# Two halves of a standing operand stored in turn, value by value, in a two-network transformer kernel

## The reference: what is computed

```python
def swiglu(h, w_gu, w_down):              # w_gu 1024 x 5632, w_down 2816 x 1024
    gate, up = jnp.split(h @ w_gu, 2, axis=-1)
    return (jax.nn.silu(gate) * up) @ w_down

def squared_relu_mlp(h, w_up, w_down):    # w_up 1024 x 4096, w_down 4096 x 1024
    return jnp.square(jax.nn.relu(h @ w_up)) @ w_down
```

## Time and profile before

| | |
|---|---|
| median of three executions | 1662.71 us (1662.34 to 1662.93) |
| profiled execution | 1661.7 us |
| its span, first to last instruction | 1660.0 us |
| mean granted TensorE clock | 0.998 |
| PE busy | 1624.5 us (98%) |
| DVE busy | 1030.6 us (62%) |
| ACT busy | 810.1 us (49%) |
| mean HBM rate | 170 GB/s |

### The profile page before, as it was taken

One profiled execution on the slowest core, in us unless ns is written; L12 is line 12 of the kernel. 1 busy time (PEld: TensorE's weight loads), 2 busy tenths in 40 slices (PEclk: granted clock), 3 DMA queues, 4 the chain that ended last, 5 costly groups with the idle time before them and its releaser, 6 DMA issues.

```text
span 1660.0 us, 25696 instructions
## 1 busy us (share of the span) xinstructions
PE 1624.5 (98%) x10390; PEld 1440.9 (87%) x10390; DVE 1030.6 (62%) x1059; ACT 810.1 (49%) x998; POOL 148.9 (9%) x117
## 2 busy tenths in 40 slices
PE   8999999999999999999999999978999999999998
PEld 6888887888889888888888998856999999889997
DVE  6554667754547654568455588766765578666564
ACT  6343567544345533456343556354544466444442
POOL 2000123300002100011000132221000000100000
PEclk9999999999999999999999999999999999999999
DMA  8545452364553554455545444321455545325551
GB/s 304 212 158 202 151 201 77 114 251 174 202 201 129 203 202 177 177 184 215 190 165 202 152 189 153 127 77 54 157 198 196 182 153 203 128 104 201 196 183 52
DMA packets 41212, 282.06 MB, mean 170 GB/s; under 512 B 4592, under 2 KB 4720, under 8 KB 7728
## 3 DMA queue, kind: packets, MB, share of 16 engines
q1 hardware_dynamic: 40752, 279.47, 45.7%
q0 software_dynamic: 384, 1.51, 0.2%
HBM read 279.91 MB, written 1.05 MB: 169 GB/s over the span
## 4 chain that ended last, share of the span: by engine, by line
PE 88%; DVE 5%; ACT 3%; POOL 2%; issue 1%; DMA 0%; SPq 0%; POOLq 0%; DVEq 0%; ACTq 0%
PE ps L393 28%; PE ps L397 27%; PE ps L396 27%; DVE w_lo L1743 1%; PE ps L597 1%; POOL arena L2489 1%; ACT arena L1578 1%; ACT arena L1576 1%; DMA raw<-weights 0%; PE ps L522 0%; PE ps L701 0%; ACT w_hi L1267 0%; ACT arena L1588 0%; DVE stat L2184 0%; PE ps L1054 0%
## 5 line engine op out<-in xcount | busy, mean ns | idle before, releaser
L1743 DVE TENSOR_TENSOR w_lo<-raw,w_hi 128x2048 fp32r<-128x2048 f32 x261 | 594.5, 2298 | 149.9 <-ACT w_hi L1267 149.8
L1267 ACT ACTIVATE w_hi<-raw 128x2048 fp32r<-128x2048 f32 x261 | 491.4, 1908 | 47.5 <-DMA raw<-weights 45.5
L393 PE MATMUL ps<-w_hi,hT 128*128 128x512 f32 (+1 forms) x984 | 384.0, 390 | 9.9 <-DVE hT L1770 7.1
L397 PE MATMUL ps<-w_hi,hT 128*128 128x512 f32 (+1 forms) x984 | 375.0, 381 | 0.0
L396 PE MATMUL ps<-w_lo,hT 128*128 128x512 f32 (+1 forms) x984 | 374.4, 380 | 0.0
L393 PE MATMUL ps<-hT,w_hi 128*128 128x256 f32 x984 | 282.3, 287 | 1.3 <-DVE hT L1770 1.2
L397 PE MATMUL ps<-hT,w_lo 128*128 128x256 f32 x984 | 277.0, 281 | 0.0
L396 PE MATMUL ps<-hT,w_hi 128*128 128x256 f32 x984 | 276.2, 281 | 0.0
L393 PEld LDWEIGHTS ps<-w_hi,hT 128*128 128x128 f32 x984 | 185.9, 189 | 44.4 <-DVE w_lo L1758 7.0
L397 PEld LDWEIGHTS ps<-w_hi,hT 128*128 128x128 f32 x984 | 185.7, 189 | 36.3
L396 PEld LDWEIGHTS ps<-w_lo,hT 128*128 128x128 f32 x984 | 186.2, 189 | 32.0 <-issue 0.7
(11 more groups left out here) (267 smaller groups left out, 1808.8 us busy)
## 6 DMA issues: line engine op xcount, KB each, us to landing
raw<-weights SPq DMA_DIRECT2D x261, 1024.0 KB, 4.8
raw<-weights SPq DMA_DIRECT2D x12, 256.0 KB, 7.1
X<-x SPq DMA_DIRECT2D x4, 256.0 KB, 6.3
out<-X SPq DMA_DIRECT2D x4, 256.0 KB, 2.1
arena<-p POOLq DMA_DIRECT2D x2, 256.0 KB, 5.6
arena<-counts POOLq DMA_DIRECT2D x1, 512.0 KB, 5.0
arena<-nsa_tables POOLq DMA_DIRECT2D x1, 448.0 KB, 6.1
const<-constants SPq DMA_DIRECT2D x1, 300.0 KB, 7.6
```

Source lines behind the costliest of these rows:

```text
L393: mm = nc.tensor.matmul(dst, a_hi, b_hi, start=start, stop=False, skip_group_check=True)
L397: return nc.tensor.matmul(dst, a_lo, b_hi, start=False, stop=stop, skip_group_check=True)
L1267: nc.scalar.activation(unit_cols(w_hi, u, 0, UNIT), raw[:, r * UNIT:(r + 1) * UNIT], ACT.Copy).then_inc(hi_done.sem, 1)
L1743: nc.vector.tensor_tensor(unit_cols(w_lo, u, 0, UNIT), raw[:, r * UNIT:(r + 1) * UNIT], f(unit_cols(w_hi, u, 0, UNIT)), ALU.subtract).then ...
```

## The change

In FFN one and FFN three, `hT` is stored with high and low half in turn: value 0 high, value 0 low, value 1 high, and so on. In the two MLPs `hid` is stored so. `hT_of` and `hid_of` return views with a step of two values (8 bytes) there. The functions `down_tiles`, `down_rows`, `down_rows_last` and the FFN's `up_rows`, as well as the writing of `hid` by ACT and DVE, now take their views from these. FFN two and four, and every other use of `hT` and `hid`, keep the halves apart. Each engine has the same instructions in the same order as before.

Two sizes change besides: `hid` is 24 values longer (and a spacer of 24 values in front of the weights is gone, so that the weights stay where they were, while `const` moves by 96 bytes), and `hT` is 56 values longer, which moves `raw`, `X`, `arena`, `sil` and `spare` by 224 bytes.

```diff
+HID_ROOM, H_ROOM = 40, 72
+H_EVERY_OTHER, HID_EVERY_OTHER = (0, 4), (9, 11)
 MOVE = 16
...
-        hid = sb("hid", 2 * HID + P + MOVE, f32r)
+        hid = sb("hid", 2 * HID + P + HID_ROOM, f32r)
         const = sb("const", NCONST)
-        sb("before_w", 24)
         w_hi, w_lo = sb("w_hi", RING * UNIT, f32r), sb("w_lo", RING * UNIT, f32r)
-        hT = sb("hT", 2 * KC * TOKENS + MOVE, f32r)
+        hT = sb("hT", 2 * KC * TOKENS + H_ROOM, f32r)
...
         def hid_of(s):
 
+            if s in HID_EVERY_OTHER:
+                return hid[:, 0:2 * HID:2], hid[:, 1:2 * HID:2]
...
         def hT_of(s):
 
+            if s in H_EVERY_OTHER:
+                return hT[:, 0:2 * KC * TOKENS:2], hT[:, 1:2 * KC * TOKENS:2]
...
-            def down_tiles(u, h, banks, first=False, last=False):
+            def down_tiles(s, u, h, banks, first=False, last=False):
+                high, rest = hid_of(s)
                 for b in banks:
                     for c in range(HC):
-                        mm = three(out_bank(b), lhs(hid_hi, h + c, b % 2), lhs(hid_lo, h + c, b % 2), unit_cols(w_hi, u, c * DM + b // 2 * 512, 512),
+                        mm = three(out_bank(b), lhs(high, h + c, b % 2), lhs(rest, h + c, b % 2), unit_cols(w_hi, u, c * DM + b // 2 * 512, 512),
...
             def ffn(s, u0):
+
+                h = hT_of(s)
...
-                            mm = three(bank(b0 + tok), lhs(hT_hi, k, tok), lhs(hT_lo, k, tok), unit_cols(w_hi, u, a, 512), unit_cols(w_lo, u, a, 512),
+                            mm = three(bank(b0 + tok), lhs(h[0], k, tok), lhs(h[1], k, tok), unit_cols(w_hi, u, a, 512), unit_cols(w_lo, u, a, 512),
...
-                    nc.scalar.activation(chunk(hid_hi, j % 2 * HC, HC), at(ACT_AT, 512), ACT.Copy).then_inc(hid_hi_done.sem, 1)
+                    nc.scalar.activation(chunk(hid_of(s)[0], j % 2 * HC, HC), at(ACT_AT, 512), ACT.Copy).then_inc(hid_hi_done.sem, 1)
...
-                    nc.vector.tensor_tensor(chunk(hid_lo, h, HC), at(ACT_AT, 512), f(chunk(hid_hi, h, HC)), ALU.subtract).then_inc(hid_split.sem, 1)
+                    nc.vector.tensor_tensor(chunk(hid_of(s)[1], h, HC), at(ACT_AT, 512), f(chunk(hid_of(s)[0], h, HC)), ALU.subtract).then_inc(hid_split.sem, 1)
```

More of the change, by code:

```diff
@@ L550, in down_tiles, with down_rows, down_rows_last @@
                         mm.then_inc(unit_used.sem, 1)
-            def down_rows(u, h, first, t=None):
+            def down_rows(s, u, h, first, t=None):
                 unit_ready(u, t)
                 pe.wait_ge(*hid_split.due(me, turn=t))
-                down_tiles(u, h, range(4), first)
-            def down_rows_last(u, h):
+                down_tiles(s, u, h, range(4), first)
+            def down_rows_last(s, u, h):
                 for i in range(2):
@@ L562, in down_rows_last @@
                     pe.wait_ge(*hid_split.due(me))
-                    down_tiles(u + i, h[i], (0, 2), last=i == 1)
-                down_tiles(u, h[0], (1, 3))
-                down_tiles(u + 1, h[1], (1, 3), last=True)
+                    down_tiles(s, u + i, h[i], (0, 2), last=i == 1)
+                down_tiles(s, u, h[0], (1, 3))
+                down_tiles(s, u + 1, h[1], (1, 3), last=True)
             def ffn(s, u0):
+                h = hT_of(s)
                 def up_rows(us, b0, fresh, t, mid):
@@ L634, in mlp @@
                 up([u0 + 2], 2, 2, None, False, mid={3: lambda: spread(7)}, h=h)
-                down_rows(u0 + 3, 0, True)
+                down_rows(s, u0 + 3, 0, True)
                 u = u0 + 4
@@ L640, in mlp @@
                         up([u + 2 * b], b % 3, 2, None, False, t, h=h)
-                        down_rows(u + 2 * b + 1, (b + 1) % 2 * HC, False, t)
+                        down_rows(s, u + 2 * b + 1, (b + 1) % 2 * HC, False, t)
                 hid_split.due(me, MLP_TURN * (MLP_TURNS - 1))
@@ L644, in mlp @@
                 up([u], 0, 2, None, False, h=h)
-                down_rows(u + 1, HC, False)
-                down_rows_last(u + 2, (0, HC))
+                down_rows(s, u + 1, HC, False)
+                down_rows_last(s, u + 2, (0, HC))
             def columns_t(us, fresh=False, mid={}):
```

## The result

| | before | after |
|---|---|---|
| median of four executions each, us | 1662.53 (1661.15 to 1662.93) | 1671.93 (1670.81 to 1674.12) |
| ratio, 95% interval | | 1.006 (1.0046 to 1.0075) |
| profiled execution, us | 1661.7 | 1670.81 |
| its span, us | 1660.0 | 1669.0 |
| mean granted clock | 0.998 | 0.997 |

The change makes the kernel 9.4 us slower. I had forecast 11.9 us less. The time lies inside my range of 1642 to 1675, but the sign is wrong.

What follows compares the result with a forecast made beforehand. PE, busy for 98% of the span, was taken as the bound. 1776 matmuls at 6.7 ns less gave 1661.7 - 11.9 = 1649.8 us, 1650.8 as a median, other terms 0; range 1642 to 1675 for 8 times in 10.

Steps and rivals of the forecast that it cites:

- My reading: 512-column matmuls: the 13.3 ns excess is the moving stream colliding with the load of the next standing operand; likeliest case 0.60.
- The step that followed from it: FFN one, three and MLPs: a load stepping 8 bytes keeps the stream's pace, collides once, then keeps its distance.
- The term of the sum: 512-column matmuls of FFN one, three and the MLPs: 6.7 ns less each, 1776 times, 11.9 us less.
- at half clock both keep their distance: Matmuls at 1.2 GHz: stream and load run at about the same pace, so the excess is gone there.
- The count: 1776 matmuls affected: FFN one and three 1056, MLPs 768, less the 48 of FFN one's first block.
- More lines, more collisions: Rival, same 1776 matmuls: the strided load touches twice as many places, 13.3 ns more each, 23.7 us, time 1686.4; chance 0.18.
- Nothing changes: Rival, 512-column streams: moving operand and array set the excess, the standing stride doesn't matter; 1662.7 us; chance 0.16.
- The load at half speed: Rival, 50 uncovered places before 512-column groups: a strided load at half speed costs 5.0 us, time 1667.7; chance 0.06.
- my sign of 200: First 256-column matmul before a 512-column group: taking 200 ns or more would show the slow load.
- The 512-column stream covers the load: 512-column matmuls: even a half-speed strided load of 218 ns stays under the 226.7 ns pitch; taken as 0.
- writing with a step is hidden: ACT and DVE writing halves: doubled time uses 1.3 of 4.1 us slack in the MLP; FFNs at most 2.6 us; taken as 0.
- the moved buffers: `const` moved 96 bytes, `arena` and neighbours 224: at most 4.1 us either way over 1366 other matmuls; taken as 0.

Runs made afterwards that it cites:

- stride_at_16: The changed kernel with `hT` and `hid` beginning 16 values further in the four stages, high and low still in turn: 1665.29 us against 1662.05 before, ratio 1.0018.
- ple_at_16: The kernel before with `hT` beginning 16 values further in the two gated projections, where it moves: 1661.03 us against 1662.05, ratio 0.9994 (0.9985 to 1.0003).
- ffn_only: The changed kernel with the stride only in `hT` of FFN one and three, `hid` as before: 1665.95 us against 1662.23 before, ratio 1.0024.
- mlp_only: The changed kernel with the stride only in `hid` of the two MLPs, `hT` as before: 1668.0 us against 1662.23 before, ratio 1.0035.
- aside_8: The changed kernel's sizes, but halves apart and contiguous, beginning 8 values further in the four stages: 1669.75 us against 1662.02 before, ratio 1.0044.
- sizes_only: The changed kernel's new sizes and moved buffers, but every half stored apart as before: 1662.57 us against 1662.23 before, ratio 1.0001.
- changed_again: The changed kernel itself, timed once more beside the kernel before: 1670.29 us against 1662.05, ratio 1.005 (1.0036 to 1.0064).
- bench_steps: Separate kernel that only streams `fp32r` matmuls, 24 of a kind, varying steps and moving offsets: 512 columns aligned 228.5 ns, with standing step 2 233.1 ns.
- bench_own_pace: Separate streaming kernel varying standing columns, moving columns, moving step and type (bf16): 512 aligned `fp32r` columns took 228.5 ns with 128 standing columns, 231.0 with 32.

## Why the prediction was wrong

**The step that failed is "My reading" at the end of the first part: the excess as a collision of the stream with the load.** The 13.3 ns are for the most part the moving stream's own: it doesn't deliver 512 `fp32r` values in less than some 226 ns, with any load. That is shown by the short load above all; the doubled pitch at a moving step of 2 and bf16 agree with it. The step that followed from it, that a load with the stride would collide once and then keep its distance, failed with it: the stream by itself has 233.1 ns with a standing step of 2, not less than its 228.5. The term of the sum was 6.7 ns less for each matmul; measured were 5.3 ns more. Each row that I read as a collision has another reading, and I didn't try it:

-, 113.3 ns for 256 columns, was my evidence that an excess of 6.7 is possible. But 113.3 is half of 226.7. It fits the same pace per column, not a smaller collision, and in `stride_at_16` twelve whole blocks run at it. Nor is it a matter of the operand's place alone, as I wrote: the same kernel has 118.6 ns at this spot in one execution and 114.2 in another. The 120 of the earlier trace rows lies above this pace; there an offset of 16 values took 2.2 ns off (`ple_at_16`).
- The earlier trace rows and the earlier trace rows: PE takes a value in 0.83 ns there, at half clock or in plain float32. The stream's own limit, 226.7 / 512 = 0.44 ns a value, isn't reached, so no excess shows. My sentence "at half clock both keep their distance" assumed a load whose pace doesn't follow the clock; it does (111.6 and 213.3 ns).

So the kernel before stood close to the floor already, and no layout of the standing operand that was tried has a 512-column pitch under it. The price of a worse place is 6.7 ns (226.7 to 233.3), and the stride gives up the good place. It is a coincidence that this equals the 6.7 ns that I had taken off, and luck that the time still fell inside my range.

**The count was right, the size came out lower.** 1776 x 6.7 = 11.9 us; found were 9.4. The 226.7 ns weren't the average before: the FFNs' runs of 42 matmuls had 229.5 ns in the mean and have 235.4 now, and the MLPs' down parts went from 228.3 and 227.0 to 232.8 and 233.7. In sum the four stages' 512-column starts grew by 9.5 us, 5.3 ns each. The 256-column parts of the FFNs became 1.5 us shorter, and 1.0 us lies elsewhere. So the traces differ by 9.0 us, and that the medians differ by the 9.4 of the 512-column matmuls alone is chance.

**The rivals.** "More lines, more collisions" (0.18) had the right sign, and its point of decision, a pitch above 226.7 in rows like the earlier trace rows, came true. Its mechanism didn't: step 0 doesn't help, and contiguous operands in `aside_8` lose as much. Its price was twice what was found (13.3 against 6.7). "Nothing changes" is refuted by `ffn_only` and `mlp_only`. "The load at half speed" is refuted: a 128-column load with a step of 2 takes 117.8 ns against 111.7, far from double. Of the 48 places where a 512-column group follows 256-column matmuls, 46 have a last short pitch of at most 121 ns (120 before). The other two, at the first down part of each MLP, took 195 and 201 ns before and take 228 and 230 now. That is above my sign of 200, but it is 0.06 us in all.

**The rules that I cited.** On the Trainium skill's "TensorE: Matmul & The Clock Gate" ("Step-by-step: what each phase is for"), that loading takes nothing from the running matmul, I wrote that the trace disagrees. In the main it was the rule that was right: the excess stays with a quarter of the load (231.0 ns against 228.5), and no layout of the standing operand that was tried won anything. But it isn't the whole: with a full load the place of the standing operand moves the pitch by 5 to 7 ns. The N/2.4 + 2.5 of the same page of the Trainium skill ("Back-to-back issue gap") is 215.8 for 512 columns; bf16 has 215.9, and no row of `fp32r` that reads each value once had a mean under 226. On the Trainium skill's "SBUF — State Buffer" ("Door 1: The DMA port swizzle"), two hits on a 16-byte line for full speed: the load by itself agrees (step 2, two values a line, 117.8 ns; step 4, one a line, 233.6). The moving operand doesn't: two values a line halve its speed (453 ns).

**What held.** The 512-column stream covers the load; writing with a step is hidden; the moved buffers cost nothing (`sizes_only`), and no wait took the place of another (PE busy for 98% of the span in both).

**Open.** Why a distance of 0 modulo 64 values is good for 512 columns and 8 or 32 is bad, why a short load gives 231.0 to 231.6 ns at the three places tried, and what besides the places moves the pitch by up to 4.5 ns from one kernel or execution to another, no run here tells. The good and the bad distances are measured; a reason in the memory would only be argued. No stream without any load was run, so a collision of a fixed size, whatever the load's length, isn't ruled out for the 4.4 ns that don't grow with the columns.

## What to carry to other kernels

Before an excess is put down to a collision of two streams, make one of them shorter and see whether the excess goes. If it stays, it isn't that one's, and a new layout of it can't give it back. Scaling the other stream with both at full length would have misled here: the excess was 13.3 ns at 256 and at 512 columns alike. A short kernel that streams 24 matmuls of each layout answers the question in one run, and its 4.6 ns times the count comes to the 8.2 us of this change (`changed_again`; 9.4 in the first measurement). And a change of layout also changes the place of the operands to each other: with 512 columns moving, an `fp32r` operand that stands at the good distance should keep it, and one that moves shouldn't be given a step.

## What the runs showed of the hardware

- An `fp32r` moving operand of 512 values that are all read once takes 226.7 to 228.5 ns at best at full clock; with 256 values read twice each, or in bf16, 215.8. A moving step of 2 or 3 values takes 453 ns and a step of 4 takes 461. With a step of 2 and each value read twice it is 227.6.
- With 512 contiguous `fp32r` columns moving and a full load, the pitch goes with the distance between moving and standing operand, which fits a count modulo 64 values (256 bytes): 226.9 to 228.5 ns in the mean at 0, 228.9 and 229.5 with the moving one 16 further, 230.6 to 237.0 at the other distances tried. With 256 columns the order is another: 119.4 to 119.5 ns at 0, 117.0 to 118.6 at the others.
- In the whole kernel the same code with the same places has had two pitches: 118.6 and 114.2 ns in two executions of the changed kernel, 113.3 and 117.8 or 232.8 and 235.7 in versions that differ elsewhere.
- A load of 128 columns, read from streams of 128 columns, takes 111.7 ns at step 1, 117.8 at step 2 and 233.6 at step 4 at full clock. At half clock it takes 213.3 ns for one value (111.6 at full) and still 233.6 at step 4.
- The granted clock fell from 1.00 to 0.50 (2.4 to 1.2 GHz) in two rows of the streams: in that of 128 columns with a standing step of 4 (`bench_steps`), where PE had one MATMUL in every 234 ns, and in that of bf16 with a moving step of 8 (`bench_own_pace`), where it had one in every 900 ns. Both pitches stayed what they were.
